# Attention by pairs of heads: weights gated and normalized before the turn, values standing in the array, three branches summed in one bank

## What is computed

```
# cut from the reference; 512 tokens, so selection and window keep every causal key
s = einsum(q, kc) * scale + bias[bucket(dist_c)]      # compressed: 31 keys
o_c = einsum(masked_softmax(s, dist_c >= 0), vc)
s = einsum(q, k_sel) * scale + bias[...]              # selected blocks
o_s = einsum(masked_softmax(s, causal), v_sel)
s = einsum(q, k_win) * scale + bias[...]              # window
o_w = einsum(masked_softmax(s, mask_w), v_win)
o = gate[0] * o_c + gate[1] * o_s + gate[2] * o_w     # gate = sigmoid(x @ w)
return o.reshape(B, Q, H * d) @ w_out
```

## Time and profile before

| | |
|---|---|
| median of 3 runs | 2220.86 us (2220.8 to 2223.72) |
| the profiled execution | 2218.89 us, its span 2217.1 us |
| PE busy | 2139.6 us (97%) |
| PEld busy | 1771.3 us (80%) |
| DVE busy | 1043.8 us (47%) |
| ACT busy | 854.7 us (39%) |
| mean granted clock of TensorE | 0.977 of full speed |

### The profile page before, as it was taken

One profiled execution on the slowest core, in us unless ns is written; L12 is line 12 of the kernel. 1 busy time (PEld: TensorE's weight loads), 2 busy tenths in 40 slices (PEclk: granted clock), 3 DMA queues, 4 the chain that ended last, 5 costly groups with the idle time before them and its releaser, 6 DMA issues.

```text
span 2217.1 us, 26303 instructions
## 1 busy us (share of the span) xinstructions
PE 2139.6 (97%) x10252; PEld 1771.3 (80%) x10252; DVE 1043.8 (47%) x1939; ACT 854.7 (39%) x1466; POOL 12.7 (1%) x24
## 2 busy tenths in 40 slices
PE   7899999999999999999999999899999999999997
PEld 5678788888878778787888888777898977888886
DVE  5536444443345345334544422564666736444323
ACT  4564333332314323333333322344767744333221
POOL 0000000000000000000000000000000000000000
PEclk9899999999999999999999999999989999999998
DMA  3212222223322222131333233422010022323331
GB/s 131 70 63 76 95 95 95 95 91 103 107 82 77 71 91 86 57 106 56 107 103 95 93 95 98 149 81 80 30 35 16 1 86 67 95 95 96 97 95 64
DMA packets 51818, 184.44 MB, mean 83 GB/s; under 512 B 5818, under 2 KB 6090, under 8 KB 51440
## 3 DMA queue, kind: packets, MB, share of 16 engines
q1 hardware_dynamic: 49248, 171.99, 23.9%
q0 software_dynamic: 2160, 10.63, 1.4%
q10 hardware_dynamic: 288, 0.15, 0.0%
HBM read 180.61 MB, written 2.14 MB: 82 GB/s over the span
## 4 chain that ended last, share of the span: by engine, by line
PE 88%; DVE 5%; ACT 4%; issue 2%; DMA 0%; SPq 0%; DVEq 0%; ACTq 0%
PE bank L380 69%; PE bank L428 6%; PE bank L783 3%; PE bank L763 2%; PE bank L666 1%; DVE WL L1255 1%; PE bank L754 1%; PE bank L777 1%; PE bank L753 1%; PE bank L656 1%; PE bank L479 1%; ACT WH L828 1%; PE bank L445 1%; DMA RAW<-in_w_in_t 0%; DVE MF L1586 0%
## 5 line engine op out<-in xcount | busy, mean ns | idle before, releaser
L380 PE MATMUL bank<-AH,WH 128*128 128x512 f32 x1648 | 654.2, 401 | 23.4 <-ACT AH L838 16.3
L1255 DVE TENSOR_TENSOR WL<-RAW,WH 128x1024 fp32r<-128x1024 f32 (+1 forms) x326 | 391.3, 1204 | 585.2 <-ACT WH L828 584.6
L380 PE MATMUL bank<-AL,WH 128*128 128x512 f32 x1648 | 644.3, 395 | 3.3 <-DVE AL L1273 3.2
L380 PE MATMUL bank<-AH,WL 128*128 128x512 f32 x1648 | 641.6, 393 | 2.4 <-DVE WL L1255 2.4
L828 ACT ACTIVATE WH<-RAW 128x1024 fp32r<-128x1024 f32 (+1 forms) x326 | 338.0, 1041 | 586.1 <-PE bank L380 503.7
L380 PEld LDWEIGHTS bank<-AH,WH 128*128 128x128 f32 x1648 | 313.4, 190 | 94.0 <-issue 21.2
L380 PEld LDWEIGHTS bank<-AL,WH 128*128 128x128 f32 x1648 | 313.4, 190 | 71.6 <-DVE AL L1273 9.5
L380 PEld LDWEIGHTS bank<-AH,WL 128*128 128x128 f32 x1648 | 313.3, 190 | 69.9 <-DVE WL L1255 3.7
L380 PE MATMUL bank<-HH,WL 128*128 128x512 f32 x528 | 205.4, 389 | 0.0
L380 PE MATMUL bank<-HH,WH 128*128 128x512 f32 x528 | 205.4, 389 | 0.0
L380 PE MATMUL bank<-HLO,WH 128*128 128x512 f32 x528 | 205.4, 389 | 0.0
(11 more groups left out here) (285 smaller groups left out, 2301.8 us busy)
## 6 DMA issues: line engine op xcount, KB each, us to landing
RAW<-in_ffn_in SPq DMA_DIRECT2D x132, 512.0 KB, 3.5
RAW<-in_ffn_out SPq DMA_DIRECT2D x48, 512.0 KB, 3.5
RAW<-in_ret_t SPq DMA_DIRECT2D x32, 512.0 KB, 3.5
RAW<-in_ffn_out SPq DMA_DIRECT2D x24, 384.0 KB, 3.0
RAW<-in_w_in_t SPq DMA_DIRECT2D x17, 512.0 KB, 3.6
RAW<-in_ret_v SPq DMA_DIRECT2D x16, 512.0 KB, 3.8
RAW<-in_ret_out SPq DMA_DIRECT2D x16, 512.0 KB, 3.6
RAW<-in_nsa_t SPq DMA_DIRECT2D x9, 512.0 KB, 3.5
```

The lines of the kernel that those rows point to most:

```text
L380: t = e.matmul(BANK[b][:, :], wt[:, sl], xx[:, kk, :], start=kk == 0 and n == 0, stop=kk == kt - 1 and n == 2)
L1255: e.tensor_tensor(WL[w][:, 0:n], RAW[r][:, 0:n], WH[w][:, 0:n], ALU.subtract).then_inc(w_low.did(v))
```

## The change

The 192 steps become 128: pair of heads f, query block i in the same order, long branch br, head of the pair hh. The differences:

- The weights are multiplied by gate / sum in SS on DVE before they are turned (`weights_of`, `weigh`), so nothing is left to scale after the values.
- In the values product the values stand (64 columns) and the turned weights stream (128 columns). Head hh writes partitions 64 hh to 64 hh + 63 of the pair's bank (4 or 5), columns of its query block; both long branches and the compressed one add into the same place. The bank then holds one feature tile of the result, and OT, its mixes and its 32 turns go. ACT and DVE split each finished bank into KHH and KLL, in slots whose keys are no longer needed, and `nsa_out` reads them there.
- The compressed branch is done once for a pair: 8 score blocks side by side in one bank (32 columns each), one bias, maximum, exponential and normalization for all 256 columns, two turns, and values products of 32 rows (VC stands four times, at partitions 0, 32, 64 and 96).
- Distances in steps grow: a step is multiplied 4 steps after its scores, turned 6 after, and its values follow 9 or 11 steps after the unit's first; SS has 8 buffers instead of 6 and PT 8 instead of 4.
- The parts of `nsa_t` stand at every second step of the first three groups, and `query` after the 16 steps of each pair. The gates are turned into their reciprocals once.

The diff, cut to what the text speaks of:

```diff
-            VC = sb("VC", [32, 4, 64], stack=ar)
+            VC = sb("VC", [128, 4, 64], stack=ar)
...
-            OT = sb("OT", [128, 4, 1024], stack=ar)
-            SS = [sb(f"SS{i}", [128, S], stack=ar) for i in range(4)] + SQ
-            PT = [sb(f"PT{i}", [128, S], stack=ar) for i in range(3)] + [ACC]
+            SS = [sb(f"SS{i}", [128, S], stack=ar) for i in range(6)] + SQ
+            PT = [sb(f"PT{i}", [128, S], stack=ar) for i in range(7)] + [ACC]
             NM = sb("NM", [128, 8], stack=ar)
             SM = sb("SM", [128, 4, 4], stack=ar)
             CF = sb("CF", [128, 4, 4], stack=ar)
+            CM = sb("CM", [128, 3, 8], stack=ar)
...
+        CS8, CD8 = T[0][:, 0:256], T[0][:, 256:512]
+        PC = [T[1][:, 256 * i:256 * i + 256] for i in range(2)]
...
-        STEPS = [(g, i, r, br) for g in range(4) for r in range(4) for i in ORDER for br in range(3)]
-        TURN, MIX = 3, 6
-        A_GROUP = len(STEPS) // 4
-
-        def cols(i, br):
-            return 7 + 8 * i if br == 0 else 128 * (i + 1)
+        STEPS = [(f, i, hh, br) for f in range(8) for i in ORDER for br in range(2) for hh in range(2)]
+        N = len(STEPS)
+        PAIR, GROUP = N // 8, N // 4
+        SCALE, TURN, FIRST, SECOND = 4, 6, 9, 11
+        LAST = N + SECOND
+        def out_at(f):
+            return max(PAIR * f + PAIR + SECOND - 4, GROUP * (f // 2) + GROUP) + 1
+        def slot(f):
+            return 4 * (f % 2) + f // 2
...
+            def small_scores(f):
+                g = f // 2
+                b = next_bank("score", (0, 1), ("small", f))
+                if f == 0:
+                    e.wait_ge(*free_v.at(("cmp", 0)))
+                for hh in range(2):
+                    e.wait_ge(*kv_a.at(("q", 2 * f + hh)))
+                    e.wait_ge(*kv_v.at(("q", 2 * f + hh)))
+                    for i in range(4):
+                        q = QHL[g % 2][:, 2 * (f % 2) + hh, i * 128:(i + 1) * 128]
+                        out_at = b[:, 128 * hh + 32 * i:128 * hh + 32 * i + 32]
+                        e.matmul(out_at, q, KCH[:, g, :], start=True, stop=False)
+                        t = e.matmul(out_at, q, KCL[:, g, :], start=False, stop=True)
+                t.then_inc(matmul.did(("small", f)))
...
+            def values(u, br):
+                f, i, _, _ = STEPS[4 * u]
+                c = 64 * (f // 2) + 256 * br
+                if br == 0 and i == ORDER[0]:
+                    enter(4 + f % 2, ("pair", f))
+                if u == 0:
+                    e.wait_ge(*free_a.at(("kv_v", 0, 3)))
+                e.wait_ge(*free_a.at(("turn", 4 * u + 2 * br + 1)))
+                for j in range(i + 1):
+                    for hh in range(2):
+                        t = e.matmul(BANK[4 + f % 2][64 * hh:64 * hh + 64, ROWS[i]], VS[:, j, c:c + 64],
+                                     PT[(4 * u + 2 * br + hh) % NPT][:, ROWS[j]], start=br == 0 and j == 0, stop=False)
+                t.then_inc(matmul.did(("values", u, br)))
+            def small_values(u):
+                f, i, _, _ = STEPS[4 * u]
+                if u == 0:
+                    e.wait_ge(*free_v.at(("cmp", 1)))
+                e.wait_ge(*free_a.at(("small turn", f)))
+                rows = slice(32 * i, 32 * i + 32)
+                for hh in range(2):
+                    t = e.matmul(BANK[4 + f % 2][64 * hh:64 * hh + 64, ROWS[i]], VC[rows, f // 2, :],
+                                 PC[f % 2][rows, 128 * hh:128 * hh + 128], start=False, stop=True)
+                t.then_inc(matmul.did(("mix", u)))
+            for s in range(LAST):
+                if s < N and s % PAIR == 0:
+                    small_scores(s // PAIR)
+                if TURN <= s < N + TURN:
+                    if (s - TURN) % PAIR == 0:
+                        small_turn((s - TURN) // PAIR)
                     turn(s - TURN)
-                if s < len(STEPS):
+                if s < N:
                     scores(s)
-                if s >= MIX:
-                    values(s - MIX)
-                g, at = s // A_GROUP, s % A_GROUP
-                if g < 3 and at < 16:
-                    part("nsa_t", 2 * g + 2 + at // 8, at % 8, A)
-            for f in range(8):
-                b = 2 + f % 4
-                enter(b, ("ot", f))
-                if f == 0:
-                    e.wait_ge(*mixed.at((len(STEPS) // 3 - 1, 2)))
-                for i in range(4):
-                    t = e.transpose(BANK[b][:, ROWS[i]], OT[:, i, f * 128:(f + 1) * 128], ident[:, :])
-                t.then_inc(matmul.did(("ot", f)))
-            three("nsa_out", (0, 1, 2), A, split_of("o"))
-            tile_by_pass("nsa_out", 3, A)
+                if s >= FIRST and (s - FIRST) % 4 == 0 and s < N + FIRST:
+                    values((s - FIRST) // 4, 0)
+                if s >= SECOND and (s - SECOND) % 4 == 0:
+                    values((s - SECOND) // 4, 1)
+                    small_values((s - SECOND) // 4)
+                if s < 3 * GROUP and s % 2 == 0:
+                    part("nsa_t", 2 + s // PAIR, s % PAIR // 2, A)
+            K = (KHH, KLL)
...
+                    if s % 4 == 0 and u >= 4:
+                        e.wait_ge(*weighed.at(("over", u - 4)))
+                    e.activation(scores, scores, ACT.Exp, bias=NM[:, s % 8:s % 8 + 1], scale=-1.0,
+                                 accum_out=SM[:, u % 4, 2 * hh + br:2 * hh + br + 1]).then_inc(exped.did(s))
+                    if s % PAIR == 0:
+                        e.wait_ge(*weighed.at(("shifted", s // PAIR)))
+                        e.activation(CD8, CD8, ACT.Exp, scale=-1.0).then_inc(exped.did(("small", s // PAIR)))
+                    if s < 3 * GROUP and s % PAIR == 0:
+                        before("nsa_t", 2 + s // PAIR)
+                    if s < 3 * GROUP and s % PAIR == PAIR - 1:
+                        query_high(2 + s // PAIR)
...
+                e.tensor_reduce(top, small, AX_X, ALU.max).then_inc(weighed.did(("top", f)))
+                e.wait_ge(*weighed.at(("top", f)))
+                if f > 0:
+                    e.wait_ge(*matmul.at(("small turn", f - 1)))
+                e.scalar_tensor_tensor(shifted, over_keys(top), GUARD, small, ALU.max, ALU.subtract).then_inc(
+                    weighed.did(("shifted", f)))
...
+                e.tensor_reduce(total, shifted, AX_X, ALU.add).then_inc(weighed.did(("total", f)))
+                e.wait_ge(*weighed.at(("total", f)))
+                if f == 0:
+                    e.wait_ge(*set_v.at("gates"))
+                e.scalar_tensor_tensor(weight, total, TINY, gates_of(f, 0, 0, 4, 48), ALU.max, ALU.mult).then_inc(
+                    weighed.did(("small over", f)))
+                e.wait_ge(*weighed.at(("small over", f)))
+                e.reciprocal(weight, weight).then_inc(weighed.did(("small weight", f)))
+                e.wait_ge(*weighed.at(("small weight", f)))
+                e.tensor_tensor(shifted, shifted, over_keys(weight), ALU.mult).then_inc(weighed.did(("small", f)))
...
+                e.scalar_tensor_tensor(c, sums4, TINY, gates_of(f, i, 1, 2, 1), ALU.max, ALU.mult).then_inc(
+                    weighed.did(("over", u)))
...
+                e.tensor_scalar(weighted, weighted, CF[:, u % 4, n:n + 1], None, ALU.mult).then_inc(weighed.did(s))
+            for s in range(LAST + 2):
+                if s < N and s % PAIR == 0:
+                    small_scores(s // PAIR)
+                if s < N:
                     biased_scores(s)
-                if s % 3 == 0 and 3 <= k < blocks + 3:
-                    mix(k - 3, 0)
-                    mix(k - 3, 1)
-                if s % 3 == 1 and 3 <= k < blocks + 3:
-                    mix(k - 3, 2)
-                if s % 3 == 1 and 2 <= k < blocks + 2:
-                    floor(k - 2)
-                if s % 3 == 2 and 2 <= k < blocks + 2:
-                    weigh(k - 2)
-                if g < 3 and at < 16 and at % 8 == 0:
-                    before("nsa_t", 2 * g + 2 + at // 8)
-                if g < 3 and at < 16 and at % 8 == 7:
-                    query(2 * g + 2 + at // 8)
-            for f in range(8):
-                e.wait_ge(*x_high.at(("o", f)))
-                e.tensor_tensor(AL[:, f, :], BANK[2 + f % 4][:, :], AH[:, f, :], ALU.subtract).then_inc(
-                    x_low.did(("o", f), ("ot", f)))
+                if s % 4 == 0 and SCALE <= s < N + SCALE:
+                    weights_of((s - SCALE) // 4)
+                if SCALE <= s < N + SCALE:
+                    weigh(s - SCALE)
+                if s < N and s % PAIR == 2:
+                    small_weights(s // PAIR)
+                if s < 3 * GROUP and s % PAIR == 0:
+                    before("nsa_t", 2 + s // PAIR)
+                if s < 3 * GROUP and s % PAIR == PAIR - 1:
+                    query(2 + s // PAIR)
+                for f in range(8):
+                    if s == out_at(f):
+                        e.wait_ge(*x_high.at(("o", f)))
```

(52 more changed lines are left out.)

199 lines of the change are left out of this document (81 added, 118 removed).

## The result

The changed kernel takes **2193.85 us** (median; 2191.96 to 2196.01) against 2220.83 (2220.64 to 2223.72): a ratio of 0.9876, 95% interval 0.9859 to 0.9893, 27 us less. 2200 was forecast, within 2174 to 2219. The profiled execution took 2193.51 us, its span is 2191.7.

A forecast was written before the change was run, and what follows sets the result against it. TensorE's own sequence, busy 97% of the span, was taken as the bound. Pairs 20.0 + loop end 4.2 - pauses 7 + clock 1.7 = 18.9 us off 2218.89 gave 2200 us, range 2174 to 2219.

The forecast's parts named there:

- Bound: Whole kernel: TensorE's matmul side is busy 97% of the span, so gains come from its own sequence, plus or minus pauses.
- Column halves at once: Values products: two heads' column halves run together, 0.0535 us a record, with bounds 0.0535 and 0.107.
- Rival A: Values products: column halves run one after the other, costing 41 us, so 2241 us; chance 0.08.
- Visits: Values products: entering and leaving smaller tile shapes costs 0.4 + 0.4 + 0.2 = 1.0 us per four steps, 4.0 a pair.
- Own sequence in all: TensorE in the attention loop: 20.0 us saved over the pairs of heads, and 4.2 us at the loop's end.
- End of the loop: Before nsa_out: the 32 turns of OT go and nsa_out does not wait for features, gaining 4.2 us.
- Pauses: PE waiting for DVE in the attention loop, mostly behind query splits: 15 us against 8.0, minus 7 us.
- DVE: DVE per pair of heads: about as loaded as before, 17 us in 21.1 (81%), so it does not bound.
- Clock: Half clock in the attention loop: seven pauses at 3.4 us each cost 12 us against 13.7, plus 1.7.
- Sum: Whole kernel: 20.0 + 4.2 - 7 + 1.7 = 18.9 us saved, giving 2200 us.
- rival D: Attention loop: visits at 0.2 us save 16 us more and pauses stay at today's 7; 2177 us, chance 0.13.
- Rival B: Attention loop: two score banks couple DVE and PE, so scores queue behind waiting weights; 16 us, 2216 us, chance 0.20.

The follow-up runs named there:

- e1: Changed kernel with both heads of a pair writing the same column half (partitions 0 to 63); 2219.5 us, 0.998 of the kernel before.
- e7: Changed kernel with compressed values on all 128 rows, zeros where other blocks' keys lie; 2193.6 us, 0.986 of the kernel before.
- e3: Changed kernel with first-branch values held until the second's (FIRST 9 to 11), one visit per unit; 2199.9 us, 0.988 of the kernel before.
- e12: e10 with first- and second-branch values together at step 12, one visit instead of two; 2169.4 us, 0.977 of the kernel before.
- e10: e8b with turns, copies and values one step later as in e9; 2176.4 us, 0.980 of the kernel before.
- e2: Changed kernel with the loop over the two heads outside the loop over tiles of values; 2204.6 us, 0.992 of the kernel before.
- e4: Changed kernel with the splitting of the next nsa_t weights six steps later on DVE and ACT; 2200.2 us, 0.990 of the kernel before.
- e9: Changed kernel with turns, copies and values one step later behind the scores; 2184.7 us, 0.983 of the kernel before.
- e6: Changed kernel with nsa_t weight splitting nine steps later and query low halves in steps 5 and 7 of the next pair; 2186.3 us, ratio 0.983.
- e11: Changed kernel with weights multiplied over the first 128 keys only, so output differs; 2186.1 us, 0.985 of the kernel before.
- e8b: e6's order together with e7's compressed values on all 128 rows; 2177.6 us, 0.980 of the kernel before.

## Why the prediction was right, point by point

- **Bound.** TensorE's own sequence decided, as said: 37.9 us less of it, 27.9 in the loop.
- **Column halves at once**: 0.0535 us a record taken, 0.0545 measured. Rival A's 41 us were right as own time (41.4 in e1), but its 2241 was not: serial halves gave 2219.5, 0.2% below the kernel before. It left out what pauses and clock give back.
- **Visits, the mis-sized term.** 1.0 us per four steps was taken from line 550; measured 0.25 + 0.25 + 0.14 = 0.64. That is 0.36 x 32 = 11.5 us. The change of shape in the middle was well put (0.2; 0.14 by e7); entering and leaving 128 by 64 tiles costs 0.25 by the starts (0.18 by e3, 0.22 by e12 against e10), not the 0.40 of four 64 by 64 tiles.
- **Own sequence in all**: 20.0 + 4.2 = 24.2 forecast, 37.9 measured. Visits are 11.5 of the 13.7; the other 2 are not located. The seventh pair, where no projection stands, shows 19.8 us of its own (25.66 less 3.0 of clock and 2.8 of pauses) where 21.1 was forecast. That is 1.3 less, no more than the visits' 0.36 four times, so the rest seems to lie in the six pairs with the products of `nsa_t`, which the prediction had cost the same.
- **End of the loop**: the 32 turns are gone and `nsa_out` starts at 1752.76 without a pause (near 1755 forecast): right.
- **Pauses**: 15 forecast, 17.4 measured. The place was right in part: those behind the query split and the compressed chain are there, 0.6 to 0.9 us where 1.5 was put. At three of the pair boundaries a second one of 1.40 us follows, behind DVE's wait for ACT's part of the `nsa_t` weights (7.4 us in all on DVE), which the prediction did not price. That the sum came so near is in part luck.
- **DVE** was put at 17 us a pair; the seventh pair shows 18.77. The pair's length, 25.66 less 3.0 for the clock, is 22.7 with 2.8 of pauses; 21 to 22 was forecast.
- **Clock**: 12 forecast ("seven pauses at 3.4 us each"), 17.0 and 18.8 measured as the prediction counts it (half of all half-clock time), 34 us at half clock where I wrote below 30. The sign was wrong: plus 1.7 forecast, minus 1.7 measured without the waits in it. Four of six stretches were 6.8 us long. The rule behind the term failed too: the stretches at 1556.6 and 1583.9 had no pause of 0.2 us or more in the 12 us before them, and the 1.40 us pause that ended at 1617.80 had no stretch behind it.
- **Sum**: 24.2 - 7 + 1.7 = 18.9 forecast; 37.9 - 8.3 - 1.7 = 27.9 measured, less 2.5 elsewhere. Too little was put on what was gained (13.7 us) and too little on what it would cost (1.3 of pauses, 3.4 of clock, 2.5 outside the loop), so half of the error cancelled, which is luck. Of rival D's case the cheaper visits came for the larger part (11.5 of 16 us), its fewer pauses did not. Rival B's mechanism exists, at 8.3 us in all, not 16 on top of 7.

## What to carry to other kernels

Price a visit to a tile shape from starts on both sides of it, and for the shape in question: here 128 by 64 tiles cost 0.25 us a visit and 64 by 64 tiles 0.40. Keep the two halves' matmuls alternating, since the overlap reached only about four records (e2).

When TensorE's own sequence shrinks by tens of microseconds, part of it comes back as pauses and half clock: 26% here (10.0 of 37.9 us), 35% between e1 and the changed kernel (14.3 of 41.4). A lever that removed own time alone (e3, e7) gave nothing while PE waited for DVE. Moving one lump of DVE's work alone made it worse (e4), and a step more of slack moved the wait from the turns to the scores (e9); together, with the split-up query and the compressed values on all rows, they took pauses from 17.4 to 12.0 (e10).

Read the granted clock of every run before a small gain is put down to an order. The medians of e6, e9 and e11 are 8 to 9 us below the changed kernel, and a clock higher by 0.004 to 0.006 is worth 5 to 10 of that; of the 25 us of e12, which ran at 0.982, it is worth 10 to 14.

## What the runs showed of the hardware

- Matmuls on the two column halves with all 128 rows overlapped fully when they alternated, 0.0545 us a record (changed kernel) against 0.109 with both heads in one half (e1). In e2's order they overlapped only about four records apart, and the second head's first record started ahead of three that stand before it in the program.
- Going from 128 by 64 tiles to 32 by 64 cost 0.10 us more than staying; streaming 128 rows instead of 32 cost nothing (e7).
- Half-clock stretches came in lengths of 3.4, 6.8 and 10.2 us in the loops of the changed kernels. Their total in the loop went from 10 to 48 us over these kernels and does not follow the sum of pauses (e2: 15.2 of pauses and 47.8 at half clock; e8b: 18.3 and 10.2). The mean granted clock of several kernels stayed close over all their runs (changed 0.972 to 0.976, e1 0.979 to 0.982, e10 0.979 to 0.982); in others it did not (e6 0.973 and 0.982, e7 0.971 to 0.981, e11 0.972 to 0.981). What draws a stretch is open; among the orders of the second round the clock differed by up to 14.1 us in the loop and the pauses by up to 9.6.
